# Ten products of constants behind the eight sums of each norm-and-add stage of a decoder step

## The reference

```
h = x + 0.5 * rmsnorm(swiglu(rmsnorm(x)))            # FFN 1, inner width 2816
a = rmsnorm(h) @ w_in
y = [conv(a) | pool(a) | sparse attention(a)] @ w_out  # the mixer
h = h + rmsnorm(y)
h = h + 0.5 * rmsnorm(swiglu(rmsnorm(h)))            # FFN 2
rmsnorm(x) = x / sqrt(mean(x*x) + 1e-6) * gain       # over the 1024 features
```

## Time and profile before

| | us |
|---|---|
| median of 3 runs | 1229.45 (1228.58 to 1230.16) |
| the profiled execution | 1233.21 |
| its span in the trace | 1231.7 |
| PE busy in it | 1127.9 (92%), 8680 records |
| DVE busy | 795.2 (65%) |
| ACT busy | 577.1 (47%) |
| POOL busy | 205.9 (17%) |
| mean granted clock of TensorE | 0.951 of full speed |

### The profile page before, as it was taken

How to read it: one execution, slowest core, us unless ns; L and a number is a source line. 1 busy time by engine, 2 the same in 40 slices (tenths; PEclk the granted TensorE clock), 3 DMA queues, 4 the chain that set the end, 5 groups by cost and what they waited for, 6 DMA issues and landing times.

```text
span 1231.7 us, 27547 instructions
## 1 busy us (share of the span) xinstructions
PE 1127.9 (92%) x8680; PEld 1069.9 (87%) x8680; DVE 795.2 (65%) x1266; ACT 577.1 (47%) x976; POOL 205.9 (17%) x229
## 2 busy tenths in 40 slices
PE   4999999899669799999889999989995789999996
PEld 4999999788548799999889999988883679999994
DVE  4666644888954766664566666467988466666547
ACT  4444434544444544443454444344554545444435
POOL 3211200200500311110132111011025021211002
PEclk9999999899879899999989999999996799999997
DMA  7455566342553255555435456642416434555541
GB/s 243 167 205 171 185 226 230 97 138 76 96 162 121 99 175 186 183 179 184 138 89 191 180 185 221 229 167 92 141 50 134 133 111 154 181 180 184 184 158 38
DMA packets 92296, 192.86 MB, mean 157 GB/s; under 512 B 12338, under 2 KB 50418, under 8 KB 92098
## 3 DMA queue, kind: packets, MB, share of 16 engines
q1 hardware_dynamic: 89730, 187.44, 46.0%
q0 software_dynamic: 2496, 4.55, 1.6%
HBM read 189.35 MB, written 2.59 MB: 156 GB/s over the span
## 4 chain that ended last, share of the span: by engine, by line
PE 50%; issue 38%; DVE 4%; POOL 4%; ACT 2%; POOLq 2%; DMA 1%; DVEq 0%; ACTq 0%; SPq 0%
PE PS L1000 15%; PE PS L1001 15%; PE PS L1002 15%; PE PS L1026 2%; PE PS L1107 1%; POOLq L1422 1%; POOL h L1389 1%; DVE w_lo L558 1%; ACT w_hi L340 1%; DVE wk L680 1%; PE PS L1089 1%; POOL vx L1423 1%; DMA raw<-in_wts 1%; DVE wk L691 0%; POOL pa L1429 0%
## 5 line engine op out<-in xcount | busy, mean ns | idle before, releaser
L558 DVE TENSOR_TENSOR w_lo<-raw,w_hi 128x1024 fp32r<-128x1024 f32 x312 | 409.2, 1312 | 314.6 <-ACT w_hi L340 312.5
L1000 PE MATMUL PS<-x_hi,w_hi 128*128 128x264 f32 x1648 | 488.6, 296 | 10.7 <-DVE w_lo L558 10.5
L1001 PE MATMUL PS<-x_lo,w_hi 128*128 128x264 f32 x1648 | 472.9, 287 | 0.0
L1002 PE MATMUL PS<-x_hi,w_lo 128*128 128x264 f32 x1648 | 472.3, 287 | 0.0
L340 ACT ACTIVATE w_hi<-raw 128x1024 fp32r<-128x1024 f32 x312 | 328.0, 1054 | 241.5 <-PE PS L1002 241.4
L1000 PEld LDWEIGHTS PS<-x_hi,w_hi 128*128 128x128 f32 x1648 | 316.9, 192 | 15.3 <-DVE w_lo L558 11.4
L1001 PEld LDWEIGHTS PS<-x_lo,w_hi 128*128 128x128 f32 x1648 | 316.9, 192 | 2.6
L1002 PEld LDWEIGHTS PS<-x_hi,w_lo 128*128 128x128 f32 x1648 | 315.0, 191 | 0.0
L1000 PE MATMUL PS<-h_hi,w_hi 128*128 (+1 forms) x832 | 237.1, 285 | 3.4 <-issue 3.0
L1002 PE MATMUL PS<-h_hi,w_lo 128*128 (+1 forms) x832 | 236.9, 285 | 0.0
L1001 PE MATMUL PS<-h_lo,w_hi 128*128 (+1 forms) x832 | 236.2, 284 | 0.0
(11 more groups left out here) (248 smaller groups left out, 930.3 us busy)
## 6 DMA issues: line engine op xcount, KB each, us to landing
raw<-in_wts SPq DMA_DIRECT2D x315, 512.0 KB, 3.7
kv<-in_kT SPq DMA_DIRECT2D x128, 64.0 KB, 2.1
kx<-in_kxT SPq DMA_DIRECT2D x128, 32.0 KB, 2.1
kv<-in_vC SPq DMA_DIRECT2D x64, 64.0 KB, 1.9
vx<-in_vC POOLq DMA_DIRECT2D x32, 64.0 KB, 2.1
vx<-in_vC SPq DMA_DIRECT2D x32, 64.0 KB, 1.9
h<-in_xT SPq DMA_DIRECT2D x1, 1056.0 KB, 4.9
out_yT<-h SPq DMA_DIRECT2D x8, 132.0 KB, 1.7
```

The source lines that it names most:

```text
L558: tt(w_lo[:, u % SPLIT, :], raw[:, u % RAW, :], w_hi[:, u % SPLIT, :].bitcast(F32), AL.subtract).then_inc(sem["w_lo"], 1)
L1000: pe.matmul(out, w_hi[:, w, cols], hi, start=start, stop=False)
L1001: pe.matmul(out, w_hi[:, w, cols], lo, start=False, stop=False)
L1002: return pe.matmul(out, w_lo[:, w, cols], hi, start=False, stop=stop)
```

## The change

Behind the eight sums of `post_sums` PE waits for `tables` and runs ten f32 products of `ones` with the cosine table into PSUM bank 2. No instruction reads their result: each opens and closes its own accumulation, and the next real product in this bank overwrites it. They raise no semaphore.

```diff
@@ post_sums
                     pe.wait_ge(sem["sq_post"], at_layer(L, "sq_post", 8 * n + d + 1))
                     pe.matmul(PS[:, 0, 0:NT], ones, sq[:, d, :],
                               start=(d == 0), stop=(d == KD - 1)).then_inc(sem["mm_post"], 1)
+                pe.wait_ge(tables, 48)
+                for _ in range(10):
+                    pe.matmul(PS[:, 2, 0:NT], ones, con[:, C_COS:C_COS + NT], start=True, stop=True)
```

## The result

The changed kernel takes 1220.6 us in the median (4 runs, 1220.21 to 1221.16), the kernel before 1229.01 us in the runs beside it (4, 1227.81 to 1230.16). The ratio on record is 0.992 (it is not the quotient of the two medians, which is 0.993), 95% interval 0.9904 to 0.9937: faster by 8.4 us by the medians, and by 7.7 to 11.8 us by the interval. The forecast was 1222.0 us. The profiled execution took 1221.16 us, its span is 1219.6 us against 1231.7.

A forecast was written before the change was run, and what follows sets the result against it. PE, busy 92% of the span, was taken as last, running cold at 1.2 GHz behind 4.8 us gaps in the norm-and-add stages. Median 1229.45 less 7.5 (7.1 + 5 x 0.09), both prices 0, gives 1222.0 us; range 1218.5 to 1227.0.

The forecast's parts named there:

- Ten products fit the gap and cost nothing: PE's gap before the squares: twenty records take at most 4.65 us of 4.80 us, ending at 224.16; cost 0.
- They hold the clock: The f32 products keep PE's clock at 1.00 through the gap, as in an 18 us f32 stretch elsewhere.
- (c): Constant operands do not count as work; the clock falls in the gap or with the real groups: 1229.5 us; 7%.
- (d): The clock falls while the added products run; cold groups start 0.9 us late in five stages: 1234 us; 5%.
- The gain is DVE's wait for the root, 7.5 us: Stages 1 to 5: DVE's idle time before the reciprocal, 7.1 us in five waits, plus 5 x 0.09 us.
- The cap by the split: DVE's split of the third weight unit, ahead of the reciprocal, is late next; only DVE's wait before it is won.
- some 0.9 us free: With a full clock, PE may start some 0.9 us after the first square (224.31) without anyone noticing.
- The rest moves along: Mixers and FFNs behind the stages hang on the reciprocal, so the whole chain moves by up to 1.9 us a stage.
- Price one: Code fetch at PE's jump at stage 3, behind the added products: against up to 1.75 us, taken as 0.
- rival (b): The code fetch at the jump stands bare: 1223.7 us, or 1225.2 with a cold stretch; 7%.
- Price two: The clock at waits behind the stages, in FFNs and mixers: between -1.5 and +1.5 us, 0 as the middle.
- Rival (a): One to three waits behind the stages bring new cold stretches, 1.5 to 4.5 us back: say 1225 us; 17%.

The follow-up runs named there:

- experiment 1: Changed kernel with each of the ten products cut from 264 columns to 8, in all six stages: 1230.04 us, ratio 0.9996 to the kernel before.
- experiment 11: Kernel before, with POOL's two transfers of the convolution and pooling states moved from each layer's start to behind its first product: 1230.5 us, ratio 0.9995.
- experiment 5: Changed kernel with the third weight unit's split on ACT and DVE moved to right behind the second's: 1221.63 us, ratio 0.9921 to the kernel before.
- experiment 4: Kernel before plus the ten products only in the stages behind FFN 2 (stages 3 and 6): 4.1 us below the kernel before, ratio 0.9965.
- 7: Changed kernel with twelve products and not ten: 1220.45 us, ratio 0.9905 to the kernel before.
- 9: Changed kernel with each sum of line 1026 issued one tile ahead, before the six products waiting for x_lo: 1218.9 us, ratio 0.9891 to the kernel before.
- 2: Kernel before plus the ten products only in the stages ahead of the mixers (stages 1 and 4): 2.4 us below the kernel before, ratio 0.9981.
- 3: Kernel before plus the ten products only in the stages behind the mixers (stages 2 and 5): 3.0 us below the kernel before, ratio 0.9976.
- 10: Changed kernel with both moves, sums one tile ahead and the third unit's split early: 1216.01 us, ratio 0.9872 to the kernel before.
- 6: Kernel before, without the ten products, with the third weight unit's split moved to right behind the second's: 1229.97 us, ratio 0.999.
- experiment 8: Changed kernel with fourteen products and not ten: 1225.57 us, ratio 0.9947 to the kernel before.
- 12: Changed kernel with five products and not ten: 1223.81 us, ratio 0.994 to the kernel before.

## Why the prediction was right, step by step

- **Ten products fit the gap and cost nothing.** Right: 219.56 to 224.17, an idle rest of 0.35 us, no instruction waits for them.
- **They hold the clock.** Right in all six stages, up to the reciprocal of line 593, and by experiment 1 it is this that counts. Rivals (c) and (d) did not come about.
- **The gain is DVE's wait for the root, 7.5 us, not the 2.6 us by which the sum moves.** Right in this pair of executions, 7.43 us in the intervals, but the size leans on the execution that it was read from. In that of experiment 11 (the kernel before but for two transfers), which stands at 1230.51 us and so nearer to the median, the intervals of the kernel without products are only 6.0 us above those of the changed one, and the FFNs behind stages 2, 3 and 5 give 1.55, 0.89 and 1.55 us more. So 7.5 from the waits alone came near to 8.4 partly by luck. The cap by the split is real but thinner than I put it. The step that failed is the start of the eighth sum: I had 232.6 from seven groups of 1.18 us, and it was 233.40 - 0.21 = 233.2 (2.0 us earlier than before and not 2.6), because I left out that a group also waits for x_lo. The root was ready only 0.37 us ahead of the split's end (experiment 5), so "some 0.9 us free" holds for PE's start, which catches up between tiles, but not for the root. It did not touch the forecast, and it spoiled my expectation of experiment 5: of the 5 to 6 us expected the six intervals gave 1.7.
- **Stage 6 gives nothing.** Right, 0.01 us.
- **The rest moves along.** Right for the FFN of stage 2 (0.01 us of difference) and roughly for the mixers (+0.91, -0.28, within what they vary by from execution to execution).
- **Price one, the jump at the layer loop.** In the changed kernel rival (b) is out: PE's first sum of stage 3 waits 0.35 us for its square like the others. In experiment 5 that sum came 0.99 us late, so 0 is not safe for every order of the work. What I left out was the other side: DVE's and ACT's stop there became shorter (by 1.35 us for DVE), and the low clock behind the fourth unit became shorter too or, in experiments 4, 5 and 7, did not come. Both belong to why experiment 4 gave 4.1 us and not 1.4. With ten or twelve products, stage 3 and the FFN behind it together took 208.5 to 210.1 us in four profiled executions (after, 4, 7 and 9), and 212.7 to 214.5 in five without (before, 1, 2, 3 and 11); fourteen products gave 211.6 and five 212.8, and the kernels with the early split 209.1 (5), 210.9 (10) and 211.8 (6, without products). Why the stop is shorter stays open. Experiment 11 rules out one cause. The weight transfers of line 239 are not ruled out. Where they start between 1.71 us ahead of the reciprocal of stage 3 and 0.07 us behind it (before, 1, 2, 3, 8, 11 and 12), it is 7.0 to 7.8 us to the fourth unit; where they start 0.3 us behind it (after, 4, 7 and 9), 5.7 to 6.4 us; where they start 6.7 us or more behind it (5, 6 and 10), 6.5 to 6.7 us. That is the first half of the rival of experiment 4. But the stop is there without them too, and no run moves these transfers alone.
- **Price two, the clock afterwards, 0 as the middle.** Rival (a) did not come about in stages 2 and 5: with products the FFN behind took 192.7 us each time but one (experiment 8). Without them I had taken a low gain of stage 5 (0.65 us) and its cold stretch for two separate accidents. They are one. In ten pairs without products (kernel before, 1, 2, 4 and 11) stage and FFN add up to 208.96 to 209.62 us, with a short stage and a long FFN or the reverse: 15.35 + 194.25 or 16.49 + 192.72. The clock shows the two forms: in stage 5 of the kernel before it falls for a short stretch in the stage and again behind the wait of 1.90 us, in stage 2 once, for longer, in the stage (0.50 from 403.90 to 410.70), and not behind it. With products it is 207.34 to 207.37 in ten pairs (the changed kernel, 3, 7, 9 and 12), and 207.62 and 209.19 with fourteen. So stages 2 and 5 are each worth about 2 us. Behind stage 3 the changed kernel did have a low clock, 0.55 from 626.50 to 630.00, but the kernel before had a longer one at that place, so it was no loss.

The gain came out at 8.4 us against 7.5: the stages about as worked out, and on top of them the loop and the clock behind stage 3 and the FFNs behind stages 2 and 5. How the 8.4 us of the medians divide among these is not shown, since only one execution of each kernel has a trace.

## What to carry to other kernels

Where a serial piece leaves TensorE idle for a few microseconds and cold behind it, products that nobody reads are a free cure if they end before its next input, and a few cost nothing even when they overrun slightly. Work the gain out not from how much earlier TensorE is, but from the idle time of the engine behind it up to what is late next. Two bounds that lie 0.4 us apart have to be moved together: each of the two moves alone bought little, both brought 0.8 us a stage. And look one part further than the stage: what the clock does at the next wait belongs to the sum (the FFN behind stage 5 took 194.25 us with a fall there and 192.71 us without).

## What the runs showed of the hardware

Products that are there as instructions but hardly work did not hold the clock here: with 20 records of 8 columns and 2.67 us idle behind them the clock was 0.50 in the next 5 us, while 10 records of 264 columns with 2.57 us idle left it at 1.00 in three of five stages. So the length of the idle stretch alone does not decide. A fall that comes late is not spared either: in stage 5 of the kernel before the whole gap of 4.80 us passed at 1.00, the clock fell to 0.51 as the work came back, and fell again to 0.50 behind a later wait of 1.90 us; behind the same wait in stage 2 it stayed at 1.00. And where the loop over layers jumps back, DVE stood 1.15 to 2.86 us on "issue" in the seven traces that name no other engine there, and ACT 0.6 to 2.3 us in all fourteen. Why it varies is not shown; it moved the time of this kernel by as much as a stage did.
